# Norm squares shared by two engines, earlier loads of the root table, convolution taps ahead of the second norm batch, and the Silu row at expert block 18

## The reference

```python
def rms_norm(x, g):                       # before every layer, and at the very end
    xf = x.astype(jnp.float32)
    y = xf * lax.rsqrt(jnp.mean(xf * xf, axis=-1, keepdims=True) + EPS)
    return (y * g.astype(jnp.float32)).astype(x.dtype)

def conformer_conv(a, b, conv_w, conv_b, norm_g):      # odd layer; C_KERNEL = 31 taps
    h = a * jax.nn.sigmoid(b)
    hp = jnp.pad(h, ((0, 0), (C_KERNEL - 1, 0), (0, 0)))
    y = lax.conv_general_dilated(hp, conv_w[:, None, :], window_strides=(1,), ...) + conv_b
    return jax.nn.silu(rms_norm(y, norm_g))

# second_block, per layer l
mod = (jax.nn.silu(c) @ ada_w[l] + ada_b[l])[:, None, :]
sh1, sc1, g1, sh2, sc2, g2 = jnp.split(mod, 6, axis=-1)
...
act = jax.nn.gelu(jnp.einsum('bcd,bchkd->bchk', hc, u_tab[ic]), approximate=False)
return jnp.einsum('bchk,bchkd->bcd', gc * act, v_tab[ic])
```

## Time and profile before

| | |
|---|---|
| median of 3 runs | 2671.34 us (2668.96 to 2673.66) |
| the profiled execution's own time | 2669.31 us |
| its span, first to last instruction | 2667.6 us |
| TensorE busy | 2375.2 us (89%) |
| VectorE busy | 1935.2 us (73%) |
| ScalarE busy | 1165.4 us (44%) |
| share of the 16 DMA engines | 45.7% |
| granted TensorE clock, mean | 0.952 |

### The profile page before, as it was taken

One profiled execution on the slowest core, in us unless ns is written; L12 is line 12 of the kernel. 1 busy time (PEld: TensorE's weight loads), 2 busy tenths in 40 slices (PEclk: granted clock), 3 DMA queues, 4 the chain that ended last, 5 costly groups with the idle time before them and its releaser, 6 DMA issues. The chain is left out here.

```text
span 2667.6 us, 38270 instructions
## 1 busy us (share of the span) xinstructions
PE 2375.2 (89%) x11686; PEld 1941.5 (73%) x11686; DVE 1935.2 (73%) x4427; ACT 1165.4 (44%) x2030; POOL 150.5 (6%) x168
## 2 busy tenths in 40 slices
PE   4797798983699899999999997889989999999996
PEld 3576456572578778888888874668878888888885
DVE  3568276545599878888888874759977777777775
ACT  3566224312315754444444433631764444444442
POOL 0000000000014400000000000002520000000000
PEclk9898898987799999999999998989999999999998
DMA  6440442164212157777767745031125555555553
GB/s 220 137 178 15 135 146 109 64 237 149 79 64 79 53 204 254 255 254 254 254 252 253 253 179 178 33 134 56 48 93 194 191 191 190 189 189 189 190 191 107
DMA packets 145273, 429.38 MB, mean 161 GB/s; under 512 B 15636, under 2 KB 22032, under 8 KB 145168
## 3 DMA queue, kind: packets, MB, share of 16 engines
q1 hardware_dynamic: 145168, 428.14, 45.7%
HBM read 427.05 MB, written 1.05 MB: 160 GB/s over the span
## 5 line engine op out<-in xcount | busy, mean ns | idle before, releaser
L2671 PE MATMUL bank<-h_t_parts,u_t_high 128*128 128x512 f32 x1824 | 450.5, 389 | 0.0
L2671 PEld LDWEIGHTS bank<-h_t_parts,u_t_high 128*128 128x128 f32 x1824 | 342.4, 188 | 71.0
L2744 ACT ACTIVATE u_t_high<-u_ring 128x1024 fp32r<-128x1024 f32 x228 | 242.0, 1061 | 178.1 <-DMA u_ring<-in_peer_u 176.9
L2685 PE MATMUL bank<-v_high,weighted_high 128*128 128x512 f32 x976 | 305.8, 395 | 9.7 <-DVE weighted_low L2804 7.4
L2764 ACT ACTIVATE activated<-activated 128x256 f32<-128x256 f32 x228 | 95.5, 419 | 480.7 <-DVE activated L2792 480.7
L2685 PE MATMUL bank<-v_low,weighted_high 128*128 128x512 f32 x976 | 303.9, 392 | 0.0
L2685 PE MATMUL bank<-v_high,weighted_low 128*128 128x512 f32 x976 | 302.4, 391 | 0.0
L2786 DVE TENSOR_TENSOR v_low<-v_ring,v_high 128x1024 fp32r<-128x1024 f32 x244 | 296.7, 1216 | 6.1 <-ACT v_high L2751 3.3
L2779 DVE TENSOR_TENSOR u_t_low<-u_ring,u_t_high 128x1024 fp32r<-128x1024 f32 x228 | 278.6, 1222 | 22.6 <-ACT u_t_high L2744 18.4
L2751 ACT ACTIVATE v_high<-v_ring 128x1024 fp32r<-128x1024 f32 x244 | 257.3, 1054 | 52.1 <-PE bank L2685 50.2
L2674 PEld LDWEIGHTS bank<-h_t_parts,u_t_low 128*128 128x128 f32 x1824 | 248.8, 190 | 17.8
(11 more groups left out here) (578 smaller groups left out, 3797.2 us busy)
## 6 DMA issues: line engine op xcount, KB each, us to landing
v_ring<-in_peer_v SPq DMA_DIRECT2D x244, 512.0 KB, 3.3
u_ring<-in_peer_u SPq DMA_DIRECT2D x228, 512.0 KB, 4.6
panel<-in_l_w_in SPq DMA_DIRECT2D x15, 2048.0 KB, 7.6
late_tiles<-in_ada_w SPq DMA_DIRECT2D x54, 512.0 KB, 4.3
mod_ring<-in_ada_w SPq DMA_DIRECT2D x42, 512.0 KB, 5.4
panel<-in_peer_w_q SPq DMA_DIRECT2D x8, 2048.0 KB, 7.8
panel<-in_l_w_out SPq DMA_DIRECT2D x4, 2560.0 KB, 8.9
early_u<-in_peer_u SPq DMA_DIRECT2D x20, 512.0 KB, 3.3
```

What stands on the lines that cost most here:

```text
L2671: nc.tensor.matmul(banks[2 + k][:, :], UTH[:, k, j, :], H2[:, j, :, :].rearrange("p a s -> p (a s)"), start=(j == 0), stop=False, skip_gro ...
L2685: last = nc.tensor.matmul(banks[4 + 2 * t + half][:, :], w[:, t * P:(t + 1) * P], v[:, k, half * 512:(half + 1) * 512], start=False, stop= ...
L2744: nc.scalar.activation(UTH[:, s, :, :].rearrange("p a b -> p (a b)"), UR[:, s, :], ACT.Copy)\
```

## The change

1. In `norm_transpose` and in the last stage ScalarE squares only tile 0; VectorE squares tile 1 in one operation with a running sum.
2. `inverse_root` has four operations in place of five, and in `norm_transpose` its last one releases ScalarE, so that the sixth goes.
3. A new helper `sqrt_table` issues a root of one column that nobody reads. It stands at the end of the stages ahead of six norms (even_out, odd_out, lru_out, mla_out, and the stage after each expert layer) and at the head of `group_roots`.
4. In odd_input the calls conv(19, 22), conv(22, 24), conv(24, 31) become conv(19, 27), conv(27, 28), conv(28, 31).
5. In the first expert layer the row silu(c) is made ahead of Gelu of block 18 and not of block 10, its load moves from behind the loads of block 7 to ahead of those of block 18, `CRAW` moves into the fourth slot of the tile ring, and the late tiles start two blocks later (22 in place of 20).

```diff
     def project(name, lhs, evac, owner, K=KD, width=None, chunks=None, ahead=3, mod_steps=0,
-                beside=None):
+                beside=None, norm_next=False):
...
+                    if who == "a" and norm_next:
+                        sqrt_table()
                 (block.scalar if who == "a" else block.vector)(body)
...
                 evacuate(f, act, "a", len(ps) - 1)
+                if norm_next:
+                    sqrt_table()
...
+    table_cells = [16]
+
+    def sqrt_table():
+
+        n = table_cells[0]
+        table_cells[0] += 1
+        nc.scalar.activation(stats[:, n:n + 1], ident[:, 0:1], ACT.Sqrt)
+
+    def inverse_root(f, v, y, t, mean_done, root_done, eng, done=None):
...
         f(nc.vector.reciprocal(y, y))
-        f(nc.vector.tensor_tensor(t, y, y, ALU.mult))
+        f(nc.vector.scalar_tensor_tensor(t, y, -0.5, y, ALU.mult, ALU.mult))
         f(nc.vector.tensor_tensor(t, t, v, ALU.mult))
-        f(nc.vector.tensor_scalar(t, t, -0.5, 1.5, ALU.mult, ALU.add))
-        f(nc.vector.tensor_tensor(y, y, t, ALU.mult))
+        return f(nc.vector.scalar_tensor_tensor(y, t, 1.5, y, ALU.add, ALU.mult), done)
...
-                for t in range(NT):
-                    f(nc.scalar.activation(xn[:, t, :], src[:, t, 0:width], ACT.Square,
-                                           accum_out=stats[:, t:t + 1]), sq_done)
+                f(nc.scalar.activation(xn[:, 0, :], src[:, 0, 0:width], ACT.Square, accum_out=stats[:, 0:1]), sq_done)
...
-                dve.wait_ge(sq_done, NT)
+                f(nc.vector.scalar_tensor_tensor(xn[:, 1, :], src[:, 1, 0:width], 1.0, src[:, 1, 0:width], ALU.mult, ALU.mult,
+                                                 accum_out=stats[:, 1:2]))
+                dve.wait_ge(sq_done, 1)
...
-                inverse_root(f, stats[:, 0:NT], stats[:, 4:4 + NT], stats[:, 8:8 + NT], mean_done, root_done, dve)
-                f(nc.vector.tensor_scalar(stats[:, 8:9], stats[:, 4:5], 1.0, None, ALU.mult), inv_done)
+                inverse_root(f, stats[:, 0:NT], stats[:, 4:4 + NT], stats[:, 8:8 + NT], mean_done, root_done, dve, inv_done)
...
         p, c = todo[0][0].shape[0], sum(src.shape[1] for src, _, _, _ in todo)
+        sqrt_table()
         eng.wait_ge(mean_done, 1)
...
-                conv(19, 22)
+                conv(19, 27)
...
-                conv(22, 24)
+                conv(27, 28)
...
-                conv(24, C_KERNEL)
+                conv(28, C_KERNEL)
...
-        CRAW = nc.alloc_sbuf_tensor_at(f"c_row{l}", [P, D], F32, offset=UT_AT)
+        CRAW = nc.alloc_sbuf_tensor_at(f"c_row{l}", [P, D], F32, offset=WORK + 3 * 4 * D)
...
-                    late[20 + 3 * n // 2].append(n)
+                    late[22 + 3 * n // 2].append(n)
+                ROW_AT = 18
...
-                        if l == 0 and b == 7:
-                            sp.wait_ge(gelued, 4)
-                            load_small(sp, [(CRAW[:, :], bcast(I["c_2"][0]))])
                     if l == 0:
                         for b in range(EARLY + 2, NB):
+                            if b == ROW_AT:
+                                sp.wait_ge(w_full, 16)
+                                load_small(sp, [(CRAW[:, :], bcast(I["c_2"][0]))])
                             step(b, b % 2)
                             for n in tiles_at(b):
+                                if n == 3:
+                                    sp.wait_ge(row_ready, 2)
...
                         if type(b) is int and b < EARLY:
-                            if l == 0 and b == EARLY - 4:
-                                act.wait_ge(small_loaded, crow_loaded)
-                                for i in range(2):
-                                    nc.scalar.activation(banks[i], CRAW[:, i * 512:(i + 1) * 512], ACT.Silu).then_inc(row_ready, 1)
-                                act.wait_ge(row_ready, 2)
                             at_least(act, weighted, b - 1)
                             nc.scalar.activation(AA[:, s, :], ACTED[:, b, :], ACT.Gelu).then_inc(gelued, 1)
                             return
+                        if l == 0 and type(b) is int and b == ROW_AT:
+                            act.wait_ge(small_loaded, crow_loaded)
+                            for i in range(2):
+                                nc.scalar.activation(banks[i], CRAW[:, i * 512:(i + 1) * 512], ACT.Silu).then_inc(row_ready, 1)
                         act.wait_ge(summed, b - EARLY + 1)
```

More of the change, by code:

```diff
@@ L2705, in _, with pipeline @@
                         step(NB - 2 + k, k, acts=k < 1, final=k == 1)
-                def pipeline(eng, split_u, split_v, other, first=lambda b, s: None, after=None):
+                def pipeline(eng, split_u, split_v, other, first=lambda b, s: None, after=None, lead=EARLY):
                     split_v(0, 0, 0)
@@ L2723, in step @@
                                 split_v(b + 1, 1 - k, lap + k)
-                    for b in range(EARLY):
+                    for b in range(lead):
                         step(b, b % 2, b // 2)
                     if after is None:
-                        with eng.Fori(EARLY // 2, NB // 2 - 1) as i:
+                        with eng.Fori(lead // 2, NB // 2 - 1) as i:
                             for k in range(2):
@@ L2762, in gelu @@
                             return
+                        if l == 0 and type(b) is int and b == ROW_AT:
+                            act.wait_ge(small_loaded, crow_loaded)
+                            for i in range(2):
+                                nc.scalar.activation(banks[i], CRAW[:, i * 512:(i + 1) * 512], ACT.Silu).then_inc(row_ready, 1)
                         act.wait_ge(summed, b - EARLY + 1)
                         nc.scalar.activation(AA[:, s, :], AA[:, s, :], ACT.Gelu).then_inc(gelued, 1)
-                    pipeline(act, split_u, split_v, gelu)
+                    pipeline(act, split_u, split_v, gelu, lead=EARLY if l else ROW_AT)
                 @block.vector
@@ L3168, in fin_act @@
         def fin_act(f, act):
-            for t in range(NT):
-                f(nc.scalar.activation(fo[:, t, :], X[:, t, :], ACT.Square, accum_out=stats[:, t:t + 1]), sq_done)
+            f(nc.scalar.activation(fo[:, 0, :], X[:, 0, :], ACT.Square, accum_out=stats[:, 0:1]), sq_done)
             act.wait_ge(mean_done, 1)
@@ L3174, in fin_dve @@
         def fin_dve(f, dve):
-            dve.wait_ge(sq_done, NT)
+            f(nc.vector.scalar_tensor_tensor(fo[:, 1, :], X[:, 1, :], 1.0, X[:, 1, :], ALU.mult, ALU.mult,
+                                             accum_out=stats[:, 1:2]))
+            dve.wait_ge(sq_done, 1)
             f(nc.vector.tensor_scalar(stats[:, 0:NT], stats[:, 0:NT], 1.0 / D, EPS, ALU.mult, ALU.add), mean_done)
```

7 lines of the change are left out of this document (3 added, 4 removed).

## The result

| | before | changed |
|---|---|---|
| median of the runs | 2672.5 us (2668.96 to 2674.11, 4 runs) | 2654.07 us (2652.01 to 2655.86, 4 runs) |
| span of the profiled execution | 2667.6 us | 2650.3 us |
| ratio | | 0.9933, 95% interval 0.9915 to 0.9950 |

A forecast was written before the change was run, and what follows sets the result against it. TensorE's gaps, chiefly the norms' one-engine-at-a-time chains, were taken to bound the kernel. Savings 10.1 + 0.4 + 0.2 + 6.5 + 1.25 + 2.3 + 1.3 = 22.0 us from 2671.3 gave 2649 us, range 2643 to 2656.

The forecast's parts named there:

- What bounds the kernel: TensorE busy 89% of the span; a microsecond less in a norm's chain is a microsecond less in the kernel.
- Squares: In each norm, one tile squared per engine starts the mean 1.05 us earlier, bounded at 0.9 and 1.18.
- Small operations: From reciprocal to scaling in each norm, four operations instead of six save 0.39 us.
- Table loads: Root's table load leaves the chain at five places, 5 x 1.30 = 6.5 us, hidden in the stages before.
- The drain: At table switches, the page's 1380 ns extra would give 6.8 us more gain, about 2642.5 us; chance 1 in 100.
- Silu row: First expert layer: TensorE's 2.27 us gap at block 10 goes; Gelu of block 18 1.3 to 1.4 late, costing nothing.
- Rival A: Block 18 stalls TensorE after all, giving 2 to 5 us back: 2651 to 2654; chance 0.07.
- Convolution: End of odd_input 1.3 us shorter, between 0 and 1.85; second batch's sums start 1.7 us late.
- The clock: TensorE's restarts at 1.2 GHz behind norms, 2.25 us each, left as they are; one or two either way.
- Rival C: Shorter gaps spare TensorE three or four restarts of 2.25 us each: 2640 to 2642; chance 0.04.
- Rivals B and D: B: recurrence's input stage gives gains back, 2659, chance 0.04; D: c_row load delays tile ring, 2677 us, chance 0.02.
- likeliest case: Whole kernel: the forecast itself, with its own range of 2645 to 2653 us; chance 0.79.

The follow-up runs named there:

- u_squares: The changed kernel with both squares of every norm on ScalarE again, 8 places; 2660.85 us.
- u_tables: The changed kernel with the helper `sqrt_table` issuing nothing, so no early root; 2657.81 us.
- u_conv: The changed kernel with the convolution cut as before (19-22, 22-24, 24-31); 2654.53 us (ratio 0.9935).
- the kernel before again: The same file as the kernel before, nothing changed, profiled for a second trace; span 2671.3 us.

## Why the prediction was right, and where it was off

- **What bounds the kernel**: right. Each norm is on the path with its full length, and undoing a part brought its length back in the norm's stage.
- **Squares**: 1.05 forecast; 1.07 measured from first square to mean, 1.06 to 1.10 by u_squares, and 1.3 at the norm of the first expert layer. That VectorE's operation would cost the same with one tile read twice, beside ScalarE, was right: 1224 ns both the earlier trace rows.
- **Small operations**: 0.39 forecast, 0.39 measured.
- **Table loads**: 5 x 1.30 forecast; 1.27 to 1.33 each by u_tables. The cover was there at all places, also in the stages after the expert blocks, for which I had no row. The drain of the Trainium skill's page "ScalarE: Activation LUTs" ("What ACT_TABLE_LOAD costs") shows neither as idle time nor as a loss when the loads were put back: five cost 6.2 us with the head norm's small operation, not 13.
- **Silu row**: the gap of 2.27 us went. At block 18 I took ScalarE to be free at 988.0 of the trace before, and the tiles of u to land 1.3 to 1.4 us early; they were being waited for already (0.82 and 0.69 us). ScalarE was held up behind a tile that had not landed. Gelu came 2.5, 2.0 and 1.9 us late in the three traces, not 1.4, and TensorE lost 0.26 us at that block in the first and nothing in the other two. Rival A happened once in three traces, and far smaller than its 2 to 5 us. The stage gave 2.5 to 2.7 us against 2.3; some 0.3 of it came without change 5.
- **Convolution**: 1.3 forecast, 1.33 by u_conv. The sums that were to start 1.7 us late were not late, because the compression had become longer.
- **The clock, and the rest that is untouched**: here the forecast was off. "I leave the restarts as they are" put this term at nothing, with one or two microseconds either way. In the traces the untouched stages lost 3.8 us in the mean and 5.2 in the first one, of which 1.0 and 1.5 are the gates' stage and not the clock. The clock's part isn't one term but many with both signs: -1.75 in the first query projection (steady, and made by the shorter norm), +1.8 in the latent stage (steady in three traces each), +1.8 in the mean in the compression, and a rest that changes with each execution. Rival C had the gain's mechanism, but in one stage instead of four. That the losses come from the change's earlier starts follows only from the comparison of before and after; no run here produced one at will, none of the edits undone brought the compression back, and what decides the clock at those two places stays open.
- **Rivals B and D** had no part: the recurrence's input stage was not longer (69.1, 70.1 and 69.4 us against 70.4, 69.4 and 69.4), and the blocks from 18 on kept their period.
- The table sums to 22.5 touched against 22.0 forecast. The closeness of the parts is the finding. The whole is 3.6 us short of the forecast, for the untouched stages lost time, the larger part of it by the clock. With that the time fell just outside the likeliest case's 2645 to 2653 and inside the wider range, which had been drawn for other reasons: that it held is in part luck. The latent norms' 0.2 was not measured by itself.

## What to carry to other kernels

Where stages meet for all engines, price an edit by the chain of its stage and check it by the length of that stage: it was right to some 0.3 us where the median of a whole run could not tell 2 us. Keep a term of up to two microseconds, of either sign, for TensorE's clock in each stage whose pause ahead changes, and profile the same kernel twice before a stretch of it is taken as its length. Look at a wait at a stage's head for all its loads: two such waits, moved to where the data are read, gave 14 us, against 18 for the whole change.

## What the runs showed of the hardware

- The same 64 small matmuls took 7.9 to 10.7 us; the mean granted clock in 10 us from about their start was 0.84 at 7.9, 0.73 at 9.7 (the kernel before again) and 0.69 at 10.3. The same norm and stage of the same kernel took 148.8 and 152.7 us in two executions.
- In the first query projection the restart behind the norm gave the stage two lengths in 13 traces, 105.7 us behind norms of 8.2 to 8.6 us and 107.5 to 108.0 behind norms of 8.9 to 10.0. In the second one the same two lengths occur, and do not follow the norm's.
- VectorE's multiply with a running sum takes 1224 ns for 128 x 1024 whether the second operand is another tile or the first again, and beside ScalarE's square of the other tile.
